# A trunk step on one core: the first tile's w2 loaded beside the weight ring, and the second turn's loads held until the second tile's rows have landed

## The reference, cut to what matters

```
act = silu(hf @ w1[e]) * (hf @ w3[e])          # D = 1024, FF = 512
y   = y + (act @ w2[e]) * comb[:, e:e + 1]     # comb: two experts per token
x   = x + g2 * moe(h);  y = rmsnorm(x)
```

## Time and profile before

| what | us |
|---|---|
| median of 3 runs | 875.78 (872.71 to 876.26) |
| the profiled execution's time | 879.9 |
| its span | 878.1 |
| PE busy | 841.1 (96%) |
| DVE busy | 685.3 (78%) |
| ACT busy | 465.6 (53%) |

### The profile page before, as it was taken

How to read it: one execution, slowest core, us unless ns; L and a number is a source line. 1 busy time by engine, 2 the same in 40 slices (tenths; PEclk the granted TensorE clock), 3 DMA queues, 4 the chain that set the end, 5 groups by cost and what they waited for, 6 DMA issues and landing times.

```text
span 878.1 us, 14907 instructions
## 1 busy us (share of the span) xinstructions
PE 841.1 (96%) x5047; PEld 699.1 (80%) x5047; DVE 685.3 (78%) x950; ACT 465.6 (53%) x556; POOL 54.5 (6%) x60
## 2 busy tenths in 40 slices
PE   7899999999999999999999999999999999999884
PEld 2499999989899999899776367888888888888650
DVE  0772647978797686698358879999899998999986
ACT  4642443333422221642223358888888888888751
POOL 0002000000000000230000010001000010000150
PEclk9999999999999999999999999999999999999996
DMA  9868544444543321223752589968997899999752
GB/s 328 277 198 283 197 119 146 146 150 162 173 131 111 96 73 49 69 82 122 254 206 92 174 302 397 398 258 321 363 354 267 315 400 399 399 397 402 263 195 97
DMA packets 90997, 201.24 MB, mean 229 GB/s; under 512 B 8792, under 2 KB 13400, under 8 KB 90918
## 3 DMA queue, kind: packets, MB, share of 16 engines
q1 hardware_dynamic: 78813, 165.25, 53.2%
q0 software_dynamic: 5136, 18.42, 5.9%
q10 hardware_dynamic: 7003, 16.95, 5.3%
HBM read 182.97 MB, written 18.35 MB: 229 GB/s over the span
## 4 chain that ended last, share of the span: by engine, by line
PE 83%; DVE 8%; DMA 3%; ACT 2%; issue 2%; ACTq 1%; SPq 1%; DVEq 0%; POOLq 0%
PE ps L799 31%; PE ps L650 12%; PE ps L652 12%; PE ps L651 12%; PE ps L879 3%; DVE w_lo L1572 2%; PE ps L994 2%; DMA region_a<-in_x_prompt_dram 2%; DMA region_b<-h_rows,slot_idx 2%; PE ps L831 2%; PE ps L1109 1%; PE ps L1113 1%; PE ps L678 1%; PE ps L679 1%; ACT w_hi L1134 1%
## 5 line engine op out<-in xcount | busy, mean ns | idle before, releaser
L1572 DVE TENSOR_TENSOR w_lo<-raw,w_hi 128x1024 fp32r<-128x1024 f32 x202 | 241.5, 1225 | 100.5 <-ACT w_hi L1134 98.6
L1134 ACT ACTIVATE w_hi<-raw 128x1024 fp32r<-128x1024 f32 x202 | 207.9, 1056 | 197.9 <-PE ps L799 150.6
L650 PE MATMUL ps<-w_hi,hT_hi 128*128 128x512 f32 (+1 forms) x512 | 206.5, 403 | 3.6 <-DVE w_lo L1572 2.7
L652 PE MATMUL ps<-w_hi,hT_lo 128*128 128x512 f32 (+1 forms) x512 | 202.7, 396 | 0.0
L651 PE MATMUL ps<-w_lo,hT_hi 128*128 128x512 f32 (+1 forms) x512 | 202.1, 395 | 0.0
L799 PE MATMUL ps<-hT_hi,w_hi 128*128 128x260 f32 x768 | 156.3, 285 | 3.3 <-DVE w_lo L1572 2.4
L799 PE MATMUL ps<-hT_hi,w_lo 128*128 128x260 f32 x768 | 155.0, 283 | 0.0
L799 PE MATMUL ps<-hT_lo,w_hi 128*128 128x260 f32 x768 | 154.8, 283 | 0.0
L799 PEld LDWEIGHTS ps<-hT_hi,w_hi 128*128 128x128 f32 x768 | 118.8, 189 | 6.5 <-DVE w_lo L1572 5.2
L799 PEld LDWEIGHTS ps<-hT_lo,w_hi 128*128 128x128 f32 x768 | 119.1, 189 | 0.0
L799 PEld LDWEIGHTS ps<-hT_hi,w_lo 128*128 128x128 f32 x768 | 118.8, 189 | 0.0
(11 more groups left out here) (328 smaller groups left out, 823.2 us busy)
## 6 DMA issues: line engine op xcount, KB each, us to landing
raw<-in_exp_w_dram SPq DMA_DIRECT2D x96, 512.0 KB
region_a<-in_exp_w_dram SPq DMA_DIRECT2D x80, 512.0 KB
raw<-in_w_in_dram SPq DMA_DIRECT2D x48, 512.0 KB
raw<-in_w_ada_dram SPq DMA_DIRECT2D x30, 512.0 KB
expert_rows<-region_b ACTq DMA_DIRECT2D x17, 512.0 KB, 6.3
region_b<-in_exp_w_dram SPq DMA_DIRECT2D x16, 512.0 KB
region_b<-in_w_ada_dram SPq DMA_DIRECT2D x14, 512.0 KB, 8.5
expert_rows<-region_a POOLq DMA_DIRECT2D x8, 512.0 KB, 8.9
```

The source lines that it names most:

```text
L650: pe.matmul(out, pairs[0], moving[0], start=start, stop=False)
L652: return pe.matmul(out, pairs[1], moving[0], start=False, stop=stop)
L1134: act.activation(w_hi[:, split_slot(n), :], place, ACT.Copy).then_inc(hi_done, 1)
L1572: return dve.tensor_tensor(out, whole, first.bitcast(F32), ALU.subtract)
```

## The change

Three things are changed. SP loads the four quarters of w2 of expert 0 (tile 0) right behind the landing of the first gather into four places of their own, `early_raw`, ahead of its read of the tables and ahead of w1 of tile 1. Turn 1 is written out ahead of the loop on SP, ScalarE and DVE: at positions 4 to 7 it sends only the marks, with no wait ahead of them, and the splits take w2 from `early_raw`. And SP's wait ahead of turn 1 is for the landing of the second gather (`xg_ready` 32), where it was for its issue (`second_begun`).

```diff
--- before.py
+++ after.py
@@ -250,6 +250,8 @@
         diag = late_raw[4][:, 0:6 * P].rearrange("p (a t) -> p a t", t=P)
         in_last = carve(region_b, 3328, CHOICES, P)
         more_raw.append(carve(region_b, 2048, QUARTER))
+
+        early_raw = [carve(region_b, at, QUARTER) for at in (9216, 10240, 0, 1024)]
         gap_place = [carve(region_b, 7168, QUARTER), carve(region_b, 8192, QUARTER), carve(region_b, 11264, QUARTER), more_raw[4],
                      carve(region_b, 6144, QUARTER), more_raw[2], more_raw[3], more_raw[5]]
         g2_rows = g2_dec[0:ND + 1, :]
@@ -362,7 +364,7 @@
         slot_idx_ready = sem("slot_idx_ready")
         table_ready = sem("table_ready")
         xg_ready = sem("xg_ready")
-        second_begun = sem("second_begun")
+        early_ready = sem("early_ready")
         gather_free = sem("gather_free")
         xgT_done = sem("xgT_done")
         silu_ready = sem("silu_ready")
@@ -615,6 +617,12 @@
             gap_load(5)
             gap_load(6)
             gap_load(7)
+            sp.wait_ge(h2T_done, NTILE)
+            sp.wait_ge(h2_stored[0], 32)
+            sp.wait_ge(h2_stored[1], 32)
+            sp.wait_ge(xg_ready, 16)
+            for q in range(KF):
+                sp.dma_start(early_raw[q], exp_w2[0, 0, q * P:(q + 1) * P, :]).then_inc(early_ready, 16)
             sp.wait_ge(table_ready, 6)
             last = sp.value_load(table[0:1, 1:2], min_val=NE - 1, max_val=MAX_TILES - 1)
             before_last = sp.value_load(table[0:1, 2:3], min_val=NE - 2, max_val=MAX_TILES - 2)
@@ -624,8 +632,13 @@
             up_weights(8, exp_w1, expert_of(slice(1, 2)), None)
             sp.dma_start(g2_bias, b_ada[0, 5 * D:6 * D].partition_broadcast(ND + 1)).then_inc(ld_mod, 16)
 
-            sp.wait_ge(second_begun, 1)
-            with sp.Fori(1, last) as j:
+            sp.wait_ge(xg_ready, 32)
+            where_fresh(up_weights, 0, exp_w3, slice(1, 2), 1, 1)
+            for q in range(4, 8):
+                _, ready, _ = raw_place(N_EXP + q)
+                sp.dma_start(kept_mark[0:1, q:q + 1], table[0:1, 0:1]).then_inc(ready, 16)
+            where_fresh(up_weights, 8, exp_w1, slice(2, 3), 1, 0)
+            with sp.Fori(2, last) as j:
                 where_fresh(up_weights, 0, exp_w3, bass.ds(j, 1), j, 1)
                 where_fresh(down_weights, 4, None, bass.ds(j - 1, 1), j, 0)
                 where_fresh(up_weights, 8, exp_w1, bass.ds(j + 1, 1), j, 0)
@@ -1124,10 +1137,10 @@
                 ins.then_inc(act_step, 1)
                 act.wait_ge(act_step, steps[0])
 
-            def hi(n, turn=None):
-
-
-                place, ready, count = raw_place(n, turn)
+            def hi(n, turn=None, early=None):
+
+
+                place, ready, count = raw_place(n, turn) if early is None else (early_raw[early], early_ready, 64)
                 act.wait_ge(ready, count)
                 if splits(n) > SPLIT or turn is not None:
                     act.wait_ge(quarter_used, splits(n) - SPLIT if turn is None else turn * TURN + (splits(n) - SPLIT))
@@ -1404,10 +1417,15 @@
             his(10, 12)
             turned_product_out(0)
             his(12, 15)
-            with act.Fori(1, last) as j:
+
+            def turn_of(j, early=False):
                 his(3, 4, j)
                 silu_tile(j)
-                his(4, 8, j)
+                if early:
+                    for q in range(KF):
+                        hi(N_EXP + 4 + q, j, q)
+                else:
+                    his(4, 8, j)
                 turned_rows_out(j + 1)
                 his(8, 11, j)
                 y_out(j - 1, TURN * j + splits(N_EXP + 7))
@@ -1415,6 +1433,10 @@
                 his(11, 12, j)
                 y_store(j, j - 1)
                 his(12, 15, j)
+
+            turn_of(1, early=True)
+            with act.Fori(2, last) as j:
+                turn_of(j)
             his(3, 4, last)
             silu_tile(last)
             his(4, 7, last)
@@ -1508,7 +1530,6 @@
             n_tiles = pool.value_load(table[0:1, 0:1], min_val=NE, max_val=MAX_TILES)
             pool.wait_ge(xgT_done, 1)
             gather(1)
-            pool.sem_inc(second_begun, 1)
             with pool.Fori(2, n_tiles) as j:
 
                 pool.wait_ge(xgT_done, j)
@@ -1571,12 +1592,13 @@
 
                 return dve.tensor_tensor(out, whole, first.bitcast(F32), ALU.subtract)
 
-            def lo(n, turn=None):
+            def lo(n, turn=None, early=None):
 
                 count = splits(n) if turn is None else turn * TURN + splits(n)
 
                 dve.wait_ge(hi_done, count)
-                rest(w_lo[:, split_slot(n), :], raw_place(n)[0], w_hi[:, split_slot(n), :]).then_inc(lo_done, 1)
+                place = raw_place(n)[0] if early is None else early_raw[early]
+                rest(w_lo[:, split_slot(n), :], place, w_hi[:, split_slot(n), :]).then_inc(lo_done, 1)
 
 
             dve.memset(cT[:, :, 16:C_LO].bitcast(F32), 0.0)
@@ -1929,7 +1951,7 @@
                     row_means(i, i, NTILE + i + 1, 3 + i)
                 if i >= 3:
                     logit_tile(i - 3)
-            dve.memset(fresh_flags[:, 0, 0:1], 1)
+            dve.memset(fresh_flags[:, 0, 0:2], 1)
             dve.memset(fresh_flags[:, 1, 0:2], 1)
             dve.tensor_copy(tile_f, tile_no[:, 0:MAX_TILES])
             dve.tensor_scalar(tile_start[:, :], tile_no[:, :], float(P), None, ALU.mult)
@@ -2006,7 +2028,7 @@
             link(dve.tensor_tensor(ended, ends[:, None, :].broadcast_to([P, MAX_TILES, NE]), tile_f[:, :, None].broadcast_to([P, MAX_TILES, NE]), ALU.is_le))
             link(dve.tensor_reduce(tile_f, ended, AX.X, ALU.add))
             dve.tensor_copy(tile_expert[:, :], tile_f).then_inc(table_ready, 1)
-            for flags, first in ((0, 1), (1, 2)):
+            for flags, first in ((0, 2), (1, 2)):
                 dve.tensor_tensor(fresh_flags[:, flags, first:], tile_f[:, first:], tile_f[:, first - 1:MAX_TILES - 1], ALU.not_equal).then_inc(table_ready, 1)
             dve.tensor_scalar(table[:, 1:2], ends[:, NE - 1:NE], -1.0, None, ALU.add).then_inc(table_ready, 1)
             dve.tensor_scalar(table[:, 2:3], ends[:, NE - 1:NE], -2.0, None, ALU.add).then_inc(table_ready, 1)
@@ -2078,16 +2100,23 @@
             link(dve.reciprocal(share[:, 0, :], col1[:, :, 4]))
             link(dve.tensor_tensor(share[:, 1, :], share[:, 0, :], col1[:, :, 5], ALU.mult), share_ready, 1)
             los(12, 15)
-            with dve.Fori(1, last) as j:
-                los(3, 7, j)
-                product_tile(j, TURN * j + splits(N_EXP + 3))
-                los(7, 8, j)
+
+            def turn_of(j, early=False):
+                los(3, 4, j)
+                for q in range(KF):
+                    lo(N_EXP + 4 + q, j, q if early else None)
+                    if q == 2:
+                        product_tile(j, TURN * j + splits(N_EXP + 3))
                 turned_rows_rest(j + 1)
 
                 list_out(bass.ds(j + 2, 1))
                 los(8, 11, j)
                 turned_product_rest(j)
                 los(11, 15, j)
+
+            turn_of(1, early=True)
+            with dve.Fori(2, last) as j:
+                turn_of(j)
             dve.wait_ge(ld_mod, 32)
             dve.wait_ge(g2_out, 2)
             dve.tensor_tensor(g2_rows, g2_rows, g2_bias, ALU.add).then_inc(g2_step, 1)
```

## The result

The changed kernel takes 880.54 us in the median (875.66 to 882.87, 20 runs), the kernel before 877.38 us (872.71 to 881.48, 20 runs). The ratio on record is 1.0028, with a 95% interval of 1.0015 to 1.0042: 2.5 us slower, between 1.3 and 3.7 (the two medians lie 3.2 us apart). The forecast of 873.6 us was wrong in sign, and the time lies above its range of 870.9 to 877.6. A change within 0.5% had been given a chance of 0.83, and 0.28% is within it, but what was forecast there was a gain. The profiled execution took 880.53 us, with a span of 878.6.

What follows compares the result with a forecast made beforehand. The loop runs at PE's pace, so only the way into it could gain, at PE's wait for the second gather. Gather 1.5 us plus clock 0.65 make 2.15 us off 875.78: 873.6 us, range 870.9 to 877.6.

Steps and rivals of the forecast that it cites:

- I take the median, 7.3 us: landing at 517.94: Second gather: 7.3 us from issue to landing in place of 8.82, a gain of 1.5 us, between 0 and 1.96.
- The clock: PE behind its wait for the second gather: no half-speed stretch with a wait of 0.4 us, a gain of 0.65 us.
- Early loads on SP: SP's queue: w1 of tile 1 issued 1.1 us later, its first quarter landing 3.2 us before ScalarE wants it; cost nothing.
- Turn 1 held until the rows land: SP's w3 of tile 1 goes out at 519.8 and lands with 1.9 down to 1.1 us of slack; cost nothing.
- the thin place: The small slack, 1.9 down to 1.1 us, of w3 of tile 1 when turn 1 is held.
- Written-out turn: Turn 1 ahead of the loop: same work in the same order on ScalarE and DVE, marks of one word; cost nothing.
- Rival 1: Second gather lands as late as before (8.8 us, 519.46), wait and slow clock stay: 875.8 us, chance 0.24.
- the slower one: Rival 4, entry of turn 1: w3 of tile 1 comes too late, 876.0 to 879.1 us, chance 0.11.
- The bound of 8.82 us: Second gather's latest landing, 519.46, taken as the end of the range where the gather's gain is 0.
- The rule: DMA engines go round robin between queues with work, so SP's queue depth wouldn't matter: gain 0 instead of 2.15 us.

Runs made afterwards that it cites:

- e1_early_only: The changed kernel with SP's turn 1 released at the second gather's issue, as before, not its landing: 881.17 us, 1.0022 of the kernel before.
- e3_after_again: The changed kernel run once more, unchanged: 880.59 us, 1.003 of the kernel before.
- f2_w1_first: The changed kernel with w1 of tile 1 issued ahead of the early w2: 882.24 us, 1.004 of the kernel before.
- h1_w2_behind: The changed kernel with the four early w2 loads moved behind the second gather's landing and w3 of tile 1: 880.04 us, 1.0008 of the kernel before.
- h2_ahead_of_first: The changed kernel with the early w2 loads let go without waiting for the first gather: 880.79 us, 1.0032 of the kernel before.
- e2_wait_only: The kernel before with only SP's wait changed, from the second gather's issue to its landing: 878.6 us, 1.0006 of the kernel before.
- g4_before_third: The kernel before, unchanged, profiled a third time for the scatter of its gather: ratio 1.0002.
- e4_quiet_gather: e2_wait_only with w1 of tile 1 held as well until the second gather lands: 883.2 us, 1.0052 of the kernel before.

## Why the prediction was wrong

**The step that failed is the gather's: "I take the median, 7.3 us: landing at 517.94".** It failed twice.

First, in the sum for the loads. The expected relief was that turn 1's w3 leaves the gather's company. But 2.1 MB of w3 issued 1.8 us behind the gather were replaced by 2.1 MB of w2 issued 6 us ahead of it. The step saw that 4.2 MB and the gather's own 0.52 MB share the engines, and had all of them moved by 518.0, at 395 GB/s from 506.0 on. By that sum even a gather that ends last lands near 518. In the changed kernel they moved from 505.5 to 519.4, at 341 GB/s. The rate of 395 GB/s was read where the engines run saturated, from 520 to 540. Behind the gather's issue they don't reach it: 257 and 325 GB/s from 510 to 514 (the windows of 2 us above), which alone makes (2 x 138 + 2 x 70)/395 = 1.05 us. The kernel before has the same fall (261 GB/s in the 3 us behind its issue), so it isn't made by the early loads; why the rate falls stays open. The landing then comes 0.45 us behind the last packet, which the sum left out. So the median of the loop's gathers stood in for a gather that ended with the last of 4.7 MB: with four early quarters beside it, the gather took 9.0 to 9.5 us in four profiles of four (after, e1_early_only, e3_after_again, f2_w1_first). It took 8.6 us with three, 7.0 and 7.5 with two and the hold, 6.5 and 6.9 with none and the hold, and 4.3 with no load beside it. That this is the bytes queued ahead, and not the places or the written-out turn, is shown by h1_w2_behind and h2_ahead_of_first, which keep both and move only the loads (6.5 and 6.8 us, one profile each); that it isn't SP's wait, by e1_early_only.

Second, in the base. The 8.82 us of the earlier trace rows were taken as what the kernel before costs. Its four profiles with the same loads have 8.8, 7.2, 6.6 and 7.8 us. So there were 0.3 us to win on average down to my 7.3, and not 1.5; with 9.0 us, the mean of after, e1_early_only and e3_after_again, 1.4 us were lost. The four and the three don't overlap, but the spread of the four leaves the 1.4 us uncertain by about 0.4 (the standard deviation of their first stretches, 0.84 us, over the root of four). The first stretch says the same: (15.40 + 15.39 + 15.49)/3 - (15.04 + 13.58 + 13.10 + 14.24)/4 = 15.43 - 13.99 = 1.4 us.

**The clock: "I expect the clock to stay at 2.4 GHz", 0.65 us.** Wrong together with the wait: granted clock 0.50 in 522 to 524, the lower of the two levels. Behind a wait for the second gather of 1.97 us or more the traces show such a half-speed stretch in four profiles of five (not in e1_early_only, which waited 2.21 us), behind 1.72 us or less in none. In the second stretch the profiles with one that otherwise run as usual (before, after, e3_after_again) need 16.6 to 16.8 us, those without one 16.2 (but for e2_wait_only, where w3 was late). So the size was about 0.45 us and the direction right, but the kernel before has it in one profile of four and the changed one in two of three, e1_early_only counted: on these few profiles it adds about 0.2 us.

**"Early loads on SP … cost nothing".** Their issue costs what was worked out, and w1 of tile 1 was not waited for. What they cost is paid by another queue's transfer, and this step priced only SP's own loads.

**"Turn 1 held until the rows land … Cost nothing".** Right in the changed kernel (e1_early_only against it: no difference), though w3 went out at 521.44 and not at 519.8. ScalarE did not wait for it near 525. This was the thin place without the early loads: in e2_wait_only the ring is short.

**"Written-out turn … Cost nothing".** Held within what can be told: 1.0003, and 0.1 us around the span.

**The rivals.** Rival 1, the gather as late as before, is what the first profile alone would suggest (9.07 against 8.82), at 0.24. Against the mean of before it is not "as late" but 1.4 us later, and no rival had that: the slower one hung on w3, which nobody waited for. The bound of 8.82 us as the longest possible was the gap: it was the largest of 18 gathers in one execution, and I took it for the largest that the changed kernel could have. In g4_before_third, the unchanged kernel, one gather of the loop took 9.5 us.

**The rule.** In the 2 us from the gather's first packets, the queues of the changed kernel (first) and of the kernel before (second) share the engines like this (packets, MB, share):

```profile
q0 software_dynamic: 106, 0.42, 51.3%
q1 hardware_dynamic: 207, 0.40, 51.1%
```

```profile
q0 software_dynamic: 103, 0.40, 62.0%
q1 hardware_dynamic: 162, 0.31, 40.1%
```

Neither queue waits until the other is empty. The Trainium skill states turns, packet by packet, between the rows with work ("DMA: Bandwidth & Descriptors", Queues, rings and completion order). The trace agrees that both have their turns; one recorded packet of each in turn it doesn't show, since q1 has twice as many as q0 in the changed kernel. By the rule alone the sum would have been 0, nearer than my 2.15. What goes beyond it in the runs is the time around this stretch. In the changed kernel no packet of q0 is recorded before 515.5, 4.7 us behind the issue. Without any load beside it (e4_quiet_gather) they begin 1.9 us behind the issue, with two early quarters 3.7 us, in the kernel before 4.0 us in the first profile and 3.4 to 3.6 in the others. And the last 0.10 MB took as long as the 0.42 MB before them. The next 1.9 us of the changed kernel, 517.5 to 519.4, read:

```profile
q1 hardware_dynamic: 203, 0.38, 52.7%
q0 software_dynamic: 38, 0.10, 14.6%
```

**What the sum is now.** Gather 1.4 us, half-speed stretch 0.2, around the span 0.1, and 14 turns of 252.65 us against a mean of 252.47 in the four profiles with the loads of the kernel before, 0.2: 1.9 us, against the measured 2.5 (1.3 to 3.7). In single runs the time also goes with the mean granted clock, by 0.41 to 0.46 us per 0.001 (slope within each kernel's runs, without and with those of the kernel before); with 0.43 the means, brought to a clock of 0.985, are 878.4 us for the kernel before, 879.6 and 880.2 for the changed one in its two samples, and 879.8 for e1_early_only. That is 1.2 to 1.8 us, and the rest would come with a slightly lower clock of the changed kernel (mean 0.9834, against 0.9847 of the kernel before in 105 runs of the later sets; for its 20 runs of the result no clock is on record). This goes together, and isn't shown to be a cause. Why it is lower stays open, and so does why the loop has two paces, 252.28 and 252.65 us for 14 turns: two of the four profiles with the loads of the kernel before have each, all with three or four early quarters the longer one, all with two the shorter. The two paces show no wait of PE that tells them apart.

The base of the median was off as well: 875.78 us from three runs, 877.38 from twenty. That is 1.6 of the 6.9 us between forecast and result; the other 5.3 us are the 2.15 us that didn't come and a loss of about 3.2 in the medians. The upper bound of the range left no room for this: with 877.38 us for the kernel before, no change at all would already lie within 0.3 us of it.

## What to carry to other kernels

When a small transfer is on the critical path, count the bytes that will stand in the other queues when it is issued, not only those issued beside it: filling an idle DMA stretch just ahead of it makes it later, and an "earlier" load is paid by someone else's landing. Compare a moved load with when the queue would have run dry: two of the four quarters cost nothing that the runs can tell, four cost 0.3%, and three lay between. And don't count on the saturated rate for the whole stretch: here the rate fell short of it by a third, then a fifth, just when the gather was issued.

A wait that depends on one transfer has a spread. Take the size of such a term from several profiles of the same program, or bound it by their spread, before subtracting from it, and don't take the longest one seen for a bound.

## What the runs showed of the hardware

The same gather of 128 rows, 0.52 MB, takes 4.3 us with no load beside it. With SP's later loads held, it takes 6.5 to 6.9 us with 2.1 MB in the queue ahead of it, 7.0 to 7.5 with 3.1 MB, 8.6 with 3.7 MB and 9.0 to 9.5 with 4.2 MB (9.05 in e1_early_only, without the hold). More than half of this growth from 4.3 to 9.1 us lies between issue and first packet (1.9 to 4.7 us), where I had looked for all of it in the transfer. In the loop, among saturated loads, the first packet comes 4.4 us behind the issue (median of 16 gathers of the changed kernel).

In the 3 us behind the issue of the second gather the DMA engines of the changed kernel moved 259 GB/s at a busy share of 0.91, with loads queued; from 780 to 820 us, in the loop, they moved 400 at a share of 1.04. A high busy share didn't mean a high rate.

Unchanged programs with the same loads spread by 2.2 us in this one gather (6.6 to 8.8), though 35 runs of the kernel before lie within 1% of each other (874.61 to 882.64 in one set).
